# Six of the 22 unit pairs of each up projection by seven half-wide block products

## The reference

```python
def conv_ffn(xn, w_up, conv_w, w_down):
    up = xn @ w_up
    a, g = jnp.split(up, 2, axis=-1)
    a = causal_dwconv(a, conv_w)
    return (jax.nn.silu(a) * g) @ w_down
```

## Time and profile before

| | us |
|---|---|
| median of 3 runs | 2099.42 |
| lowest, highest | 2099.3, 2099.99 |
| span of the profiled execution, first to last instruction | 2098.1 |
| TensorE busy in it | 2090.3 |
| VectorE, ScalarE, GpSimd busy | 972.7, 884.3, 1164.5 |

### The profile page before, as it was taken

One profiled execution on the slowest core, in us unless ns is written; L12 is line 12 of the kernel. 1 busy time (PEld: TensorE's weight loads), 2 busy tenths in 40 slices (PEclk: granted clock), 3 DMA queues, 4 the chain that ended last, 5 costly groups with the idle time before them and its releaser, 6 DMA issues.

```text
span 2098.1 us, 29633 instructions
## 1 busy us (share of the span) xinstructions
PE 2090.3 (100%) x9860; PEld 1709.4 (81%) x9860; DVE 972.7 (46%) x1682; ACT 884.3 (42%) x1355; POOL 1164.5 (56%) x1554
## 2 busy tenths in 40 slices
PE   9999999999999999999999999999999999999999
PEld 7788888888888888888888888888777778888887
DVE  6567564334455551234445544213377755545300
ACT  5544556223434343332244344224466655434321
POOL 8553346556555556555455656565544536556653
PEclk9999999999999999999999999999999999999999
DMA  6333222323332333323233333333322213333332
GB/s 234 119 99 114 63 64 70 106 78 123 92 100 93 96 94 102 95 91 100 91 101 100 96 94 89 108 94 101 111 81 81 81 61 101 100 100 90 103 92 76
DMA packets 62667, 203.70 MB, mean 97 GB/s; under 512 B 7056, under 2 KB 8720, under 8 KB 62576
## 3 DMA queue, kind: packets, MB, share of 16 engines
q1 hardware_dynamic: 60624, 201.54, 30.9%
q10 hardware_dynamic: 1952, 0.99, 0.2%
HBM read 199.42 MB, written 2.26 MB: 96 GB/s over the span
## 4 chain that ended last, share of the span: by engine, by line
PE 98%; DVE 1%; DMA 0%; DVEq 0%; ACT 0%; issue 0%; ACTq 0%; SPq 0%
PE bank L1652 28%; PE bank L1654 28%; PE bank L1653 28%; PE bank L1992 1%; PE bank L2018 1%; PE bank L1761 1%; PE bank L2004 1%; PE bank L1706 1%; PE bank L1965 1%; PE bank L1967 1%; PE bank L1966 1%; PE bank L1891 1%; PE bank L1889 1%; PE bank L1890 1%; PE bank L2049 1%; PE bank L1802 1%
## 5 line engine op out<-in xcount | busy, mean ns | idle before, releaser
L519 POOL TENSOR_TENSOR WL<-RAW,WH 128x256 fp32r<-128x256 f32 x1424 | 1105.8, 809 | 865.7 <-ACT WH L655 858.8
L1652 PE MATMUL bank<-XH,WH 128*128 128x512 f32 x1688 | 661.2, 392 | 0.3 <-DVE FG L1571 0.3
L1654 PE MATMUL bank<-XH,WL 128*128 128x512 f32 x1688 | 657.2, 389 | 0.0
L1653 PE MATMUL bank<-XL,WH 128*128 128x512 f32 x1688 | 656.9, 389 | 0.0
L655 ACT ACTIVATE WH<-RAW 128x1024 fp32r<-128x1024 f32 (+1 forms) x366 | 372.9, 1023 | 236.1 <-PE bank L1654 208.4
L1652 PEld LDWEIGHTS bank<-XH,WH 128*128 128x128 f32 x1688 | 316.9, 188 | 68.4 <-issue 2.8
L1654 PEld LDWEIGHTS bank<-XH,WL 128*128 128x128 f32 x1688 | 316.9, 188 | 66.7
L1653 PEld LDWEIGHTS bank<-XL,WH 128*128 128x128 f32 x1688 | 317.0, 188 | 64.5
L1652 PE MATMUL bank<-FH,WH 128*128 128x512 f32 x528 | 205.4, 389 | 0.0
L1653 PE MATMUL bank<-FL,WH 128*128 128x512 f32 x528 | 205.4, 389 | 0.0
L1654 PE MATMUL bank<-FH,WL 128*128 128x512 f32 x528 | 205.4, 389 | 0.0
(11 more groups left out here) (336 smaller groups left out, 2618.5 us busy)
## 6 DMA issues: line engine op xcount, KB each, us to landing
RAW<-in_w_up SPq DMA_DIRECT2D x132, 512.0 KB, 3.5
RAW<-in_w_att SPq DMA_DIRECT2D x50, 512.0 KB, 3.6
RAW<-in_w_down SPq DMA_DIRECT2D x48, 448.0 KB, 3.2
RAW<-in_w_down SPq DMA_DIRECT2D x24, 512.0 KB, 3.5
RAW<-in_w_ain SPq DMA_DIRECT2D x24, 512.0 KB, 3.4
RAW<-in_w_fa SPq DMA_DIRECT2D x24, 512.0 KB, 3.6
RAW<-in_w_mrg SPq DMA_DIRECT2D x15, 512.0 KB, 3.9
RAW<-in_w_mrg SPq DMA_DIRECT2D x24, 256.0 KB, 2.7
```

The source lines that it names most:

```text
L519: last = nc.gpsimd.tensor_tensor(WL[:, s, w], RAW[:, s, w], WH[:, s, w].bitcast(F32), ALU.subtract)
L1652: mm(dst[:, 0:width], WH[:, s, w], a, start=start and k == 0, stop=False)
L1653: mm(dst[:, 0:width], WH[:, s, w], b, start=False, stop=False)
L1654: last = mm(dst[:, 0:width], WL[:, s, w], a, start=False, stop=stop and k == kc - 1)
```

## The change

In each up stage, pairs 4, 6, 8, 10, 12 and 14 (of 22, counted from 0) are computed in a form of Strassen's scheme. A pair's weights are two units by two halves of the input features (a11, a12, a21, a22, each a *quarter* of 512 columns); the input has two halves of features by two halves of positions. Seven products of 4 blocks by 256 positions, each of them with three matmuls a block, take the place of eight. Four need differences of input blocks: ScalarE makes XG (x times the gain) at the start of the stage, VectorE the differences XD and their low parts TL, ScalarE the high parts TH; they lie in the part of the FH and FL space that later pairs fill. Four weights are sums, which VectorE writes over RAW after the plain quarters have been split. High and low parts of the seven weight quarters go into WH and WL of slots s0 and s1 and three quarters of s2 and s3, which the next, normal pair needs too. VectorE puts the outputs together from seven half banks, FIRST (a copy of product 1) and RUN. The first pairs and those between are unrolled; a loop is left for the last six pairs. Loads are issued in the same order as before.

The core of the diff (the small helpers `part`, `high`, `whole`, `hi_quarter`, `first_out`, `glu`, `second_out` and `diff_lo` hold what the loops held; the stages "up1" and "up2" are changed as "up0" is):

```diff
+PAIR0 = 4
+NWINO = 6
+HM = S // 2
+HK = KB // 2
+TAIL0 = (PAIR0 + 2 * NWINO) // 2
...
+    XG = at("XG", 56, [P, KB, S])
+    XD = at("XD", 72, [P, 4, HK, HM])
+    TL = at("TL", 72, [P, 4, HK, HM], F32R)
+    TH = at("TH", 28, [P, 4, HK, HM], F32R)
+    FIRST, RUN = SQ[:, 0:HM], SQ[:, HM:S]
...
+    WP = {1: bank[2][:, 0:HM], 2: bank[3][:, 0:HM], 5: bank[4][:, 0:HM], 4: bank[5][:, 0:HM],
+          6: bank[6][:, 0:HM], 3: bank[2][:, HM:S], 7: bank[3][:, HM:S]}
...
+        def low_quarter(s, h, s_raw, h_raw):
+            for c in range(2):
+                w = slice(h * UW // 2 + c * 2 * P, h * UW // 2 + (c + 1) * 2 * P)
+                r = slice(h_raw * UW // 2 + c * 2 * P, h_raw * UW // 2 + (c + 1) * 2 * P)
+                last = nc.gpsimd.tensor_tensor(WL[:, s, w], RAW[:, s_raw, r], WH[:, s, w].bitcast(F32), ALU.subtract)
+            return last
+        def up_lows(name, l):
+            for j in range(2 * PAIR0):
+                lo(U[name], j, 0, 0)
+            s0, s1, s2, s3 = up_slots(name)
+            for i in range(NWINO):
+                w = NWINO * l + i
+                u = U[name] + 2 * (PAIR0 + 2 * i)
+                pool.wait_ge(w_hi, 5 * w + 1)
+                low_quarter(s1, 0, s1, 1).then_inc(w_lo, 1)
+                pool.wait_ge(w_hi, 5 * w + 2)
+                low_quarter(s0, 0, s0, 0).then_inc(w_lo, 1)
+                pool.wait_ge(w_hi, 5 * w + 3)
+                low_quarter(s0, 1, s0, 1).then_inc(w_lo, 1)
+                pool.wait_ge(w_hi, 5 * w + 4)
+                low_quarter(s1, 1, s1, 1).then_inc(w_lo, 1)
+                pool.wait_ge(w_hi, 5 * w + 5)
+                low_quarter(s2, 1, s0, 0).then_inc(w_lo, 1)
+                pool.wait_ge(half_hi, 2 * w + 1)
+                low_quarter(s2, 0, s2, 0)
+                pool.wait_ge(hi_ready, u + 1)
+                low_quarter(s3, 0, s0, 1).then_inc(lo_ready, 1)
+                pool.wait_ge(hi_ready, u + 2)
+                low_quarter(s3, 1, s1, 0).then_inc(lo_ready, 1)
+                pool.wait_ge(hi_ready, u + 3)
+                low_quarter(s2, 1, s2, 1).then_inc(lo_ready, 1)
+                pool.wait_ge(half_hi, 2 * w + 2)
+                low_quarter(s3, 0, s3, 0)
+                pool.wait_ge(hi_ready, u + 4)
+                low_quarter(s3, 1, s3, 1).then_inc(lo_ready, 1)
+            los(name, 11, 4, TAIL0)
...
-        los("up0", 11, 4)
+        up_lows("up0", 0)
...
+            u0 = U[name]
+            whole(u0 + 3)
+            for k in range(KB):
+                A_(XG[:, k, :], X[:, k, :], ACT.Identity, scale=col(gain, k)).then_inc(xg_ready, 1)
+            part(0, 0)
+            whole(u0 + 4)
+            high(0, 0)
+            whole(u0 + 5)
+            diff_hi(0, 0)
+            diff_hi(1, 2)
+            part(0, 1)
+            whole(u0 + 6)
+            high(0, 1)
+            whole(u0 + 7)
+            diff_hi(2, 1)
+            diff_hi(3, 3)
+            part(1, 0)
+            high(1, 0)
+            s0, s1, s2, s3 = up_slots(name)
+            for i in range(NWINO):
+                w = NWINO * l + i
+                m = PAIR0 + 2 * i
+                u = u0 + 2 * m
+                act.wait_ge(unit_done, u - 2)
+                act.wait_ge(raw_full[s1], 16 * ((u + 1) // NSLOT + 1))
+                hi_quarter(s1, 0, s1, 1).then_inc(w_hi, 1)
+                act.wait_ge(raw_full[s0], 16 * (u // NSLOT + 1))
+                hi_quarter(s0, 0, s0, 0).then_inc(w_hi, 1)
+                hi_quarter(s0, 1, s0, 1).then_inc(w_hi, 1)
+                if i:
+                    high(0, m - 2)
+                act.wait_ge(w_sum, 4 * w + 1)
+                hi_quarter(s1, 1, s1, 1).then_inc(w_hi, 1)
+                act.wait_ge(w_sum, 4 * w + 3)
+                act.wait_ge(unit_done, u - 1)
+                hi_quarter(s2, 1, s0, 0).then_inc(w_hi, 1)
+                part(0, m - 1)
+                act.wait_ge(raw_full[s2], 16 * ((u + 2) // NSLOT + 1))
+                hi_quarter(s2, 0, s2, 0).then_inc(half_hi, 1)
+                act.wait_ge(w_sum, 4 * w + 4)
+                act.wait_ge(unit_done, u)
+                hi_quarter(s3, 0, s0, 1).then_inc(hi_ready, 1)
+                hi_quarter(s3, 1, s1, 0).then_inc(hi_ready, 1)
+                high(0, m - 1)
+                act.wait_ge(w_prod, 3 * w + 1)
+                A_(FIRST, WP[1], ACT.Copy).then_inc(w_copy, 1)
+                act.wait_ge(w_prod, 3 * w + 3)
+                hi_quarter(s2, 1, s2, 1).then_inc(hi_ready, 1)
+                act.wait_ge(raw_full[s3], 16 * ((u + 3) // NSLOT + 1))
+                act.wait_ge(unit_done, u + 1)
+                hi_quarter(s3, 0, s3, 0).then_inc(half_hi, 1)
+                act.wait_ge(unit_done, u + 2)
+                hi_quarter(s3, 1, s3, 1).then_inc(hi_ready, 1)
+                part(0, m)
...
+            first_out(0, 0)
+            dve.wait_ge(xg_ready, KB * l + HK)
+            diff(0, b12, b11)
+            dve.wait_ge(xg_ready, KB * l + KB)
+            diff(2, b22, b12)
+            second_out(0, 0)
+            first_out(0, 1)
+            diff(1, b22, XD[:, 0, :, :])
+            dve.drain()
+            diff(3, b21, XD[:, 1, :, :])
+            diff_lo(0, 0)
+            diff_lo(1, 2)
+            second_out(0, 1)
+            first_out(0, 2)
+            diff_lo(2, 1)
+            diff_lo(3, 3)
+            second_out(0, 2)
...
+            def weight_sums(w):
+                dve.wait_ge(w_lo, 5 * w + 1)
+                v.tensor_tensor(a22, a21, a22, ALU.add).then_inc(w_sum, 1)
+                dve.wait_ge(w_lo, 5 * w + 2)
+                dve.drain()
+                v.tensor_tensor(a21, a11, a21, ALU.subtract).then_inc(w_sum, 1)
+                dve.drain()
+                v.tensor_tensor(a11, a22, a11, ALU.subtract).then_inc(w_sum, 1)
+                dve.wait_ge(w_lo, 5 * w + 3)
+                dve.drain()
+                v.tensor_tensor(a12, a12, a11, ALU.subtract).then_inc(w_sum, 1)
+            def pair_first(w, m):
+                dve.wait_ge(w_copy, w + 1)
+                dve.wait_ge(w_prod, 3 * w + 2)
+                v.tensor_tensor(TA[:, 0:HM], WP[2], FIRST, ALU.add).then_inc(lin_free, 1)
+                dve.wait_ge(w_prod, 3 * w + 3)
+                v.tensor_tensor(RUN, WP[6], FIRST, ALU.add)
+                dve.drain()
+                v.tensor_tensor(TA[:, HM:S], WP[5], RUN, ALU.add)
+                dve.wait_ge(unit_done, U[name] + 2 * m + 1)
+                dve.drain()
+                v.tensor_tensor(TA[:, HM:S], WP[3], TA[:, HM:S], ALU.add)
+                dve.drain()
+                v.tensor_tensor(TA[:], TA[:], R[:], ALU.mult)
+                dve.drain()
+                conv3(TA, taps, m, bias, off).then_inc(conv_ready, 1)
+            def pair_second(m):
+                dve.wait_ge(unit_done, U[name] + 2 * m + 2)
+                v.tensor_tensor(RUN, WP[7], RUN, ALU.add)
+                dve.drain()
+                v.tensor_tensor(TE[:, 0:HM], WP[4], RUN, ALU.add)
+                v.tensor_tensor(TE[:, HM:S], WP[5], RUN, ALU.add).then_inc(lin_free, 1)
+                dve.drain()
+                v.tensor_tensor(TE[:], TE[:], R[:], ALU.mult)
+                dve.drain()
+            for i in range(NWINO):
+                w = NWINO * l + i
+                m = PAIR0 + 2 * i
+                if i:
+                    pair_second(m - 2)
+                    glu(0, m - 2)
+                weight_sums(w)
+                first_out(0, m - 1)
+                second_out(0, m - 1)
+                pair_first(w, m)
...
+            body(1, False)
+            for n in range(NWINO):
+                m = PAIR0 + 2 * n
+                wino(name, wino_of, n)
+                for j in range(2 * m + 2, 2 * m + 4):
+                    pe.wait_ge(lin_free, O[name] + j + 1)
+                    unit(U[name], j, 0, 0, KB, xh, xl, 0, LB[(O[name] + j) % 2])
...
+        def wino(name, l, n):
+            w = NWINO * l + n
+            m = PAIR0 + 2 * n
+            u, o = U[name] + 2 * m, O[name] + 2 * m
+            s0, s1, s2, s3 = up_slots(name)
+            def product(dst, s, h, xh, xl):
+                for k in range(HK):
+                    c = slice(h * UW // 2 + k * P, h * UW // 2 + (k + 1) * P)
+                    mm(dst, WH[:, s, c], xh[:, k, :], start=k == 0, stop=False)
+                    mm(dst, WH[:, s, c], xl[:, k, :], start=False, stop=False)
+                    last = mm(dst, WL[:, s, c], xh[:, k, :], start=False, stop=k == HK - 1)
+                return last
+            pe.wait_ge(lin_free, o)
+            pe.wait_ge(w_lo, 5 * w + 2)
+            product(WP[1], s0, 0, XH[:, 0:HK, 0:HM], XL[:, 0:HK, 0:HM]).then_inc(w_prod, 1)
+            pe.wait_ge(w_lo, 5 * w + 3)
+            product(WP[2], s0, 1, XH[:, HK:KB, 0:HM], XL[:, HK:KB, 0:HM]).then_inc(w_prod, 1)
+            if n == 0:
+                pe.wait_ge(xd_lo, 4 * l + 4)
+            pe.wait_ge(w_lo, 5 * w + 4)
+            product(WP[5], s1, 1, TH[:, 0, :, :], TL[:, 0, :, :])
```

(49 more changed lines are left out.)

88 lines of the change are left out of this document (58 added, 30 removed).

## The result

The changed kernel takes 2152.67 us (median of 4 runs, 2152.03 to 2153.20), the kernel before 2099.36 us beside it: 53.3 us more, a ratio of 1.0253 with a 95% interval of 1.0239 to 1.0268. The forecast of 2155 us, slower, came true, and 2152.67 lies inside its range. The profiled execution has a span of 2151.3 us.

What follows compares the result with a forecast made beforehand. TensorE's matmuls bound the kernel before; a dependency ring through VectorE, ScalarE and GpSimd would bound changed rounds. 2098.1 + 1.3, 15 us less for matmuls, 63 more for waits, 8 more at stage entries: 2155 us, range 2120 to 2186.

Steps and rivals of the forecast that it cites:

- TensorE's part: Changed pairs: 84 matmuls of 256 columns replace 48 of 512, 0.84 us less a pair, 15 us less in all.
- the rival of half-wide products that are not cheaper: Changed pairs: weight loads not hidden behind matmuls of 256 columns, 5.1 us more a pair, 2199 us; chance 3%.
- what I costed at nothing: Loads into RAW slots and unrolled code in place of loops: no added time.
- The ring: From one product 3 to the next through VectorE, ScalarE, GpSimd: 24.4 us against 20.92 of matmuls; 63 us more.
- The unslowed sum: Chain between successive products 3 with nothing slowed beside GpSimd: 21.57 us, against 20.92 us of matmuls.
- the weight of two thirds for the slowing: GpSimd is beside VectorE two thirds of a round, so 24.4 us was taken between 21.57 and 25.94.
- the rival of a ring that never closes: Changed rounds stay under 20.92 us, TensorE remains the bound, 2087 us; chance 8%.
- taken at its worst: Each of 12 two-operand VectorE operations waits out a GpSimd operation of 0.738 us: round about 30 us, time 2260 us.
- What I called usual: VectorE operations with two SBUF operands (line 1438) beside GpSimd: slowing of 0.42 us usual, at most 0.6.
- The entry: Start of each stage: unit 5 waits for a bank VectorE frees late, 2, 2 and 4 us, together 8.
- a fall after each gap: Clock at 1.2 GHz after each wait before product 3, 1.43 us more each, 26 us, 2181 us; chance 9%.
- a sign of being wrong: VectorE's operations from product 3 to normal convolution under 15 us, TensorE waiting elsewhere, or stage clock below 1.00.

Runs made afterwards that it cites:

- the run with the light GpSimd: Changed kernel with GpSimd's low quarters cut to an eighth of their columns, except first half of s2 and product 3's weights: 2093.54 us, 2093.47 in the second run.
- 12 pairs: Every third pair changed, four a stage, with weights of products 3 and 7 and copy of product 1 earlier, against the kernel before: 2099.92 us, ratio 1.0002.
- the earlier weights: Changed kernel with high and low parts of the weights of products 3 and 7 made before the normal pair's activation and first half of s2: 2135.39 us.

## Why the prediction was right

**TensorE's part.** 15 us forecast, 13.8 measured alone. The pace of 0.12 us is in the timeline above, and a round without a ring wait lasts 20.98 us (10.07 and 10.91) against 20.92 forecast. So the rival of half-wide products that are not cheaper was wrong, and what I costed at nothing (loads, unrolled code) cost nothing that TensorE's waits show.

**The ring.** Its place, its releaser and its order came out as forecast: product 3, released by GpSimd, once for every changed pair. Two runs that take a piece out of it open it, one that adds a piece pays for it in full, one that reorders it moves the wait to the next thing. The round is 24.09 us where I took 24.4. Step by step, from the timelines above (forecast's two ends in brackets):
- product 3 and its signal, 1150.22 to 1152.00: 1.78 us (1.65);
- rest of `pair_first`, to 1156.51: 4.51 (3.92 to 4.83);
- `pair_second`, to 1158.61: 2.10 (2.46 to 2.88), the one step well outside its ends;
- `glu`, to 1161.61: 3.00 (2.71 to 3.13);
- four sums, to 1166.04: 4.43 (3.27 to 4.95);
- first output, to 1169.70: 3.66 (3.39 to 3.88);
- ScalarE, to 1170.93: 1.23 (1.25);
- GpSimd and its signal, to 1174.31: 3.38 (2.92 to 3.37).

**The size of its lower end was wrong.** The unslowed sum of 21.57 us was too long. In the run with the light GpSimd the same steps last 1.71, 3.43, 2.10, 2.28, 2.96 and 3.01 us; with ScalarE's 1.23 and 3.2 to 3.4 us for GpSimd's four operations and a signal, it is some 20 us, an estimate, as the ring doesn't close there. Drain gaps are the main cause: I took 0.17 us, and between the sums 0.08 us lies (1162.76 + 1.06 to 1163.90), likewise in `pair_second`. In `glu` I had also taken slowed rows for unslowed ones: FL at 0.92 and ScalarE's trip at 0.93 us, which are 0.69 and 0.70 in that run. These errors and the weight of two thirds for the slowing cancel: the slowing is worth 24.1 - 20 = 4.1 us, nearly all that lay between my two ends (4.37), not two thirds of it. That 24.4 came so near to 24.09 is therefore luck; the ring itself is not. So the rival of a ring that never closes was nearer than I said: it fails by GpSimd's presence alone. My strongest argument against it, that even the unslowed sum is too long, was false.

**The slowing.** An operation with two SBUF operands goes from 0.69 to 1.05 us, 0.36 more; the rule in the Trainium skill (SBUF — State Buffer, Who interferes with whom), taken at its worst, would have added a whole GpSimd operation, 0.73 us or more, to each. The trace sides with the rows that I went by: about half of that. What I called usual, 0.42 us, was one row of 1.11 us in the earlier trace rows; in the kernel before the median of that line is only 0.14 us above its least, and it is in the changed rounds that 0.36 is usual. GpSimd is slowed as well: its operations of 256 columns have a median of 0.918 us in the changed pairs and 0.738 in the earlier trace rows.

**The entry.** 8 us forecast (bounds 2 to 11), 5.5 us of waits measured, released by VectorE's TE as forecast. The longest, 2.4 us, is in the third stage, where I had put 4; the clock falls behind it, which costs 1.6 us more. With the steps about the waits it is 8.1 us in all (see the account), so the 8 came out with a term for the clock that I didn't have:

```profile
1801.20:1803.60 2.40, 2.40 (x7) 1.82 (x7) 1.61 (x3) 1.68 (x3) 1.31 (x3) 0.50 0.00 0
```

**The clock.** I gave 9% to a fall after each gap and 26 us, and named a granted clock below 1.00 in the stages as a sign of being wrong. That sign is there: the clock falls, though not after each gap and not at that price. Behind the wait that ends at 621.28 TensorE runs at half of the clock, the 1.2 GHz level, and then at 2.4 GHz again (windows of the changed kernel):

```profile
618.00:621.20 3.20, 0.40 (x4) 0.19 (x2) 1.65 (x4) 2.17 (x5) 3.20 (x5) 1.00 0.00 0
621.30:622.80 1.50, 1.50 (x13) 1.50 (x14) 0.59 (x2) 0.00 (x0) 1.50 (x3) 1.00 0.33 85
622.90:626.20 3.30, 3.30 (x16) 3.11 (x15) 2.92 (x4) 1.26 (x2) 3.03 (x4) 0.50 0.79 253
626.50:629.00 2.50, 2.50 (x13) 2.05 (x12) 2.28 (x5) 1.34 (x3) 1.84 (x3) 1.00 0.52 206
```

Seven of the 18 gaps are followed by such a stretch, and one wait at the third stage's entry. Each of the seven makes the matmuls 1.5 us slower (22.72 against 21.21 us busy in the two rounds above), but more than half of this is free. In that round the next wait shrinks from 2.88 to 1.39 us, because the ring sets the round:

```profile
1198.42 0.36 PE L2192 MATMUL bank<-XH,WH 128*128 128x256 f32 x1 [1.39 <-POOL WL L578]
```

Four rounds, where the fall reached product 3 itself, are 0.2 to 1.2 us longer, 2.9 us in all with two that grow by less than 0.1; the seventh fall, behind the last round of the first stage, costs its 1.5 us. The Trainium skill (TensorE: Matmul & The Clock Gate, Why this matters for your kernels) warns of such gaps; that they open the way to a fall agrees with the rows; of the seven times 1.5 us that they took, 4.4 were paid here, where the loop waits for something else.

**The account.** 13.8 less, which holds the round's 20.98 us in place of 20.92; 15 rounds over 20.98 us, 49.5 more (364.2 us in all); the first products 3 of the stages 7.7; a fall behind the last round of the first stage 1.5; entry 5.5 in listed waits, 1.0 in the steps about these waits (from the matmul at 568.33 to the one at 570.44 us is 1.88 us more than the pace, for a listed 1.72, and the next step is 0.11 longer) and 1.6 for the clock. Sum 53.0 us, measured 53.3.

## What to carry to other kernels

Two engines at half of their time are no spare capacity: follow who waits for whom from one round to the next, sum that ring, and compare it with the bound engine's round. Sum it with the durations that the operations have when the engines are busy together, and check the unslowed end as well, since it decides whether the ring closes at all. A saving on the bound engine pays only in rounds whose ring is shorter, and its start-up is paid once a stage: here 9.4 us earned in 12 pairs went to the first pair of three stages.

## What was not expected of the hardware

- The slowing between VectorE and GpSimd goes both ways and by the kind of operand: two SBUF operands 0.69 to 1.05 us, scalar times tensor plus tensor 0.75 to 1.07, one tensor with scalars 0.55 to 0.81, reads from PSUM not at all (0.42, 0.69); GpSimd's operation of 256 columns from 0.74 to 1.16 (five in 5.79 us beside the sums, from 1160.93).
- Gaps of the same 3.1 to 3.2 us on TensorE were followed by a granted clock of 0.50 in six cases of eleven; a shorter one of 2.3 us (to 1247.20) was as well, one of 2.9 us (to 1876.79) wasn't. With the earlier weights none of the gaps of 1.6 to 1.8 us was, but one of 2.9 us. What decides it was not settled.
- 20 matmuls that compute nothing kept the granted clock at 1.00 through the rounds and shortened this kernel by 3.3 us.
